# Two output gates of a hybrid block computed as seven half-size products each

## The chip, the cores and the metric

The kernel runs on one core of one Trainium2 chip. The metric is the time of the whole kernel on the device, in microseconds (us), as the median of the runs made. Its engines are named as in the profile: PE is TensorE's matmul, PEld TensorE's weight load, DVE is VectorE, ACT is ScalarE, POOL is GpSimd, SP is SyncE, which here only issues transfers. "ACTq" and "SPq" are the instruction queues of ACT and SP where they issue a transfer.

## The reference

Two blocks are computed on 1024 tokens of width 1024; the change lies in the first, in its forgetting attention and in what follows it.

```python
h = _rmsnorm(x, pre_g)
proj = jnp.einsum('bld,de->ble', h, w_in)
z_ssm, xbc, dt_raw, q, k, v, f_raw, z_att, g_ssm, g_att = jnp.split(proj, _offsets(IN_SPLITS), axis=-1)
...
o = _forgetting_attention(heads(q), heads(k), heads(v), log_f)     # 16 heads of 64
y_att = (o.astype(f32) * jax.nn.silu(z_att.astype(f32))).astype(x.dtype)
p_ssm = jnp.einsum('ble,ed->bld', y_ssm, w_branch_ssm)
p_att = jnp.einsum('ble,ed->bld', y_att, w_branch_att)
merged = jax.nn.sigmoid(g_ssm) * p_ssm + jax.nn.sigmoid(g_att) * p_att
out = jnp.einsum('bld,de->ble', merged, w_out)
return x + _rmsnorm(out, post_g)
```

The two output gates of attention are `silu(z_att)` and `sigmoid(g_att)`, each `h` (1024 x 1024) times 1024 columns of `w_in`.

## The kernel before

**Precision.** Every operand is cut into a rounded high part (ACT) and the rest, the low part (DVE). A product is three matmuls: high x high, high x low, low x high.

**Memory.** On-chip memory is one arena of six regions R(0) to R(5), 8192 fp32 a partition each. `BANK` is 512 columns, `KC` is 8 blocks of 128 rows, `CH` is 4. The accumulators `ps` are 8 banks.

**Two forms of a dense product.** `phase_dense` takes jobs of 512 output columns. A job has 8 steps, one for each block of 128 rows; a step is 8 banks times three matmuls, 24 matmuls. For each step ACT rounds the weights (`_w`, 128x512) and `h` (`_t`, 128x1024), and DVE makes both low parts. `phase_units` computes 1024 columns as a unit of kind "full": seven products of half-size matrices (table `FULL`) instead of eight, in 28 steps of 12 matmuls. Sums of quadrants of `h` (`S1` to `S4`) are not made there: they lie in DRAM (`h_ops`), already cut into high and low, and SP streams one 512 KB operand a step into a ring of four buffers (`bs_a`). `load_operand(n)` waits until step n-4 is multiplied. Raw weights come as four quadrants of 1 MB (`B11`, `B21`, `B12`, `B22`); DVE makes their sums in place (`combine`), ACT rounds one quadrant row block a step (`bs_b`), DVE makes its low part, ACT copies three products out (`take`), and DVE adds four (`join`).

**Order of the stages around the change.** `bs` is a chain of units on TensorE (z_ssm, half of g_ssm, q, the branch of the state-space part, k, v), which ends with v. Its raw weights lie in R(0), its operand buffers in R(5). v is written to DRAM in four quarters by ACT's queue (`att_vh`, `att_vl`). Then comes `phase_forget_attention`: 16 heads of 12 score tiles; heads are loaded ahead by SP (`fa_a` and `fa_b` for a head, `fa_v` for two), ACT makes the exponentials and rounds them (`fa_ph`), POOL makes their low parts (`fa_pl`), TensorE multiplies with `fa_v`. While head h runs, TensorE also computes the row maxima of head h+1 and, from its eighth tile on, of head h+2 (`tops`, matmuls of `fa_a` alone), so `fa_a` of head h+2 is first read in head h. SP's queue does for head h, in this order: load a of head h+2, load b of head h+1, `keep_sums(h-1)`, for even h `load_v`, `spread_inverse(h-2)`.

Regions: `fa_v` and `fa_pl` lie in R(5), so their filling waits for the last product of `bs`. `h` had been in R(0) and was written to DRAM as `hT_kept` (4 MB) in the first stage; at h = 2 SP's queue loads it back into R(0). The stage `za` after attention is one `phase_dense` of six jobs: two for `silu`, two for `sigmoid`, two for the product with `w_branch_att`. All engines run their own instruction lists, written out by this code; nothing reorders them.

The lines that the steps of the prediction touch:

```python
            pool.wait_ge(tail.product, tail.products)      # before fa_v is filled
...
                if h == 2:
                    sp.wait_ge(tail.low, tail.steps)
                    sp.dma_start(hT, hT_kept).then_inc(h_back, 16)
```

## Time and profile before

| what | value |
|---|---|
| median of 3 runs (lowest, highest) | 2888.19 us (2883.37, 2891.59) |
| profiled execution: its time, its span | 2894.49 us, 2892.7 us |
| busy share of the span: PE, PEld | 94%, 77% |
| DVE, ACT, POOL | 68%, 51%, 18% |
| chain that ended last: PE, DMA, DVE, POOL | 51%, 13%, 8%, 6% |

TensorE is busy nearly everywhere, so a microsecond in which it idles or computes less is a microsecond of the kernel, as long as the other engines keep up. Times inside the trace count from the start of the span.

### The profile page before, as it was taken

What the parts mean: (1) busy time and instruction counts of PE and PEld (TensorE: products, weight loads), DVE (VectorE), ACT (ScalarE), POOL (GpSimd) and SP (SyncE); (2) the same over time, 40 slices, a digit from 0 to 9 for tenths busy, and PEclk for the clock granted to TensorE, in tenths of its full rate; (3) what the DMA queues carried; (4) which work ended last, traced back from release to release, by engine and by line L of the source; (5) the groups of instructions that cost most, each with busy time, mean ns of one, the idle gap of its engine ahead of it and who ended that gap; (6) DMA issues with size and microseconds to landing.
All of it is one profiled execution on the core that took longest, in us unless ns stands there. A gap on an engine that the chain in (4) does not pass through costs nothing.

```text
span 2892.7 us, 36287 instructions
## 1 busy us (share of the span) xinstructions
PE 2731.9 (94%) x13214; PEld 2237.7 (77%) x13214; DVE 1961.8 (68%) x2336; ACT 1467.5 (51%) x2228; POOL 519.7 (18%) x394
## 2 busy tenths in 40 slices
PE   7999999999988999999989998999999899999996
PEld 6788978788766777888878877778778788888875
DVE  6776756565654653435544987899763799888885
ACT  5544436443335664443333457533422477777774
POOL 0001400000126773001000000000010044334431
PEclk9999999999999999999999999999999899999998
DMA  5712066743786762121211100112232799999995
GB/s 173 261 49 73 1 194 244 279 157 132 278 243 173 155 137 62 51 102 44 96 58 47 51 23 1 37 44 68 78 104 81 270 381 377 375 362 369 362 360 170
DMA packets 189469, 471.85 MB, mean 163 GB/s; under 512 B 74353, under 2 KB 74481, under 8 KB 164496
## 3 DMA queue, kind: packets, MB, share of 16 engines
q1 hardware_dynamic: 166112, 427.86, 43.5%
q10 hardware_dynamic: 14000, 25.30, 2.4%
q0 software_dynamic: 9216, 16.81, 2.3%
q8 instruction: 89, 1.46, 0.2%
q14 instruction: 52, 0.43, 0.0%
HBM read 410.84 MB, written 75.83 MB: 168 GB/s over the span
## 4 chain that ended last, share of the span: by engine, by line
PE 51%; DMA 13%; DVE 8%; POOL 6%; issue 5%; ACT 4%; SPq 0%; POOLq 0%; DVEq 0%; ACTq 0%; PEldq 0%
PE ps L906 7%; PE ps L908 7%; PE ps L907 7%; DMA ex_raw<-in_w_up_e 6%; POOL fa_pl L1938 6%; DMA ex_raw<-in_w_down_e 5%; PE ps L1354 5%; PE ps L1356 5%; PE ps L1357 5%; PE ps L3515 3%; DVE ex_w L3665 3%; ACT ex_w L3600 2%; PE ps L3243 1%; PE ps L2618 1%; PE ps L2276 1%
## 5 line engine op out<-in xcount | busy, mean ns | idle before, releaser
L3665 DVE TENSOR_TENSOR ex_w<-ex_raw,ex_w 128x2048 fp32r<-128x2048 f32 x190 | 430.6, 2289 | 64.6 <-ACT ex_w L3600 62.3
L3600 ACT ACTIVATE ex_w<-ex_raw 128x2048 fp32r<-128x2048 f32 x190 | 361.9, 1916 | 112.9 <-DMA ex_raw<-in_w_up_e 63.0
L3515 PE MATMUL ps<-ex_w,ex_xT 128*128 128x512 f32 x1536 | 368.0, 396 | 12.6 <-DVE ex_xT L3680 12.3
L3515 PEld LDWEIGHTS ps<-ex_w,ex_xT 128*128 128x128 f32 x1536 | 286.8, 189 | 79.2 <-issue 14.0
L798 DVE SCALAR_TENSOR_TENSOR arena<-arena,small 128x1023 f32<-128x1023 f32 (+9 forms) x168 | 213.4, 1270 | 3.7
L1938 POOL TENSOR_TENSOR fa_pl<-fa_p,fa_ph 128x512 fp32r<-128x512 f32 x192 | 196.3, 1040 | 84.6 <-ACT fa_ph L2040 82.8
L1480 DVE TENSOR_TENSOR bs_b<-arena,bs_b 128x512 fp32r<-128x512 f32 x160 | 110.3, 690 | 139.5 <-ACT bs_b L1378 139.2
L1378 ACT ACTIVATE bs_b<-arena 128x512 fp32r<-128x512 f32 x160 | 100.1, 629 | 201.6 <-PE ps L1357 180.0
L3515 PE MATMUL ps<-ex_w,ex_hT 128*128 128x512 f32 x768 | 184.2, 396 | 1.3 <-issue 1.0
L3515 PEld LDWEIGHTS ps<-ex_w,ex_hT 128*128 128x128 f32 x768 | 142.8, 189 | 31.6 <-issue 2.6
L1755 DVE TENSOR_REDUCE small<-ps 128x1 f32<-128x512 f32 (+1 forms) x192 | 101.1, 553 | 84.6 <-PE ps L1734 56.4
L906 PE MATMUL ps<-gb_t,gb_w 128*128 128x512 f32 x368 | 146.3, 398 | 11.5 <-DVE gb_w L1005 3.7
L1014 DVE TENSOR_TENSOR za_t<-arena,za_t 128x1024 fp32r<-128x1024 f32 x48 | 60.1, 1252 | 142.4 <-ACT za_t L967 142.3
L906 PE MATMUL ps<-za_t,za_w 128*128 128x512 f32 x368 | 145.0, 394 | 5.7 <-DVE za_t L1014 3.3
L2030 ACT ACTIVATE fa_p<-ps 128x512 f32<-128x512 f32 x192 | 94.1, 491 | 101.6 <-PE ps L1972 48.8
L908 PE MATMUL ps<-gb_t,gb_w 128*128 128x512 f32 x368 | 144.6, 393 | 0.0
L907 PE MATMUL ps<-gb_t,gb_w 128*128 128x512 f32 x368 | 144.5, 393 | 0.0
L907 PE MATMUL ps<-za_t,za_w 128*128 128x512 f32 x368 | 144.1, 392 | 0.0
L908 PE MATMUL ps<-za_t,za_w 128*128 128x512 f32 x368 | 143.9, 391 | 0.0
L1354 PE MATMUL ps<-bs_a,bs_b 128*128 128x512 f32 x352 | 138.1, 392 | 4.7 <-DMA bs_a<-h_ops 3.5
L1356 PE MATMUL ps<-bs_a,bs_b 128*128 128x512 f32 x352 | 137.5, 391 | 0.0
L1357 PE MATMUL ps<-bs_a,bs_b 128*128 128x512 f32 x352 | 137.4, 390 | 0.0
(466 smaller groups left out, 6688.8 us busy)
## 6 DMA issues: line engine op xcount, KB each, us to landing
ex_raw<-in_w_gate_e SPq DMA_DIRECT2D x64, 1024.0 KB, 13.8
ex_raw<-in_w_up_e SPq DMA_DIRECT2D x64, 1024.0 KB, 13.6
ex_raw<-in_w_down_e SPq DMA_DIRECT2D x64, 1024.0 KB, 14.1
bs_a<-h_ops SPq DMA_DIRECT2D x100, 512.0 KB, 4.2
arena<-in_w_in SPq DMA_DIRECT2D x72, 512.0 KB, 3.7
arena<-in_w_in SPq DMA_DIRECT2D x18, 1024.0 KB, 6.8
h_ops<-ko_s SPq DMA_DIRECT2D x16, 512.0 KB, 6.1
h_ops<-xbc_t SPq DMA_DIRECT2D x16, 512.0 KB, 4.0
```

What stands on the lines that cost most here:

```text
L798: ins = dve.scalar_tensor_tensor(out=acc[:, b, back:], in0=src[:, b, 0:SEQ - back], scalar=w, in1=acc[:, b, back:], op0=ALU.mult, op1=ALU.add)
L906: nc.tensor.matmul(c.ps[:, t, :], a[0], b[0], start=(k == 0), stop=False)
L907: nc.tensor.matmul(c.ps[:, t, :], a[0], b[1], start=False, stop=False)
L908: mm = nc.tensor.matmul(c.ps[:, t, :], a[1], b[0], start=False, stop=(n == last[j]))
L1354: nc.tensor.matmul(to, w[0], moving[0], start=(k == 0 and fresh), stop=False, skip_group_check=True)
L1356: nc.tensor.matmul(to, w[0], moving[1], start=False, stop=False, skip_group_check=True)
L1357: mm = nc.tensor.matmul(to, w[1], moving[0], start=False, stop=closes, skip_group_check=True)
L1480: tt(b_slot[n % NB][:, 1, :], place_of[rows[u][x][1]][:, k, :], b_slot[n % NB][:, 0, :].bitcast(F32), ALU.subtract).then_inc(low, 1)
L1938: nc.gpsimd.tensor_tensor(low[x % 4][:, 0:w], prob[x % 3][:, 0:w], f32(high[x % 4][:, 0:w]), ALU.subtract).then_inc(lowered, 1)
L3515: mm = nc.tensor.matmul(out, l, r, start=(k == 0 and n == 0), stop=(k == kc - 1 and n == 2))
L3600: nc.scalar.activation(half_of(part[m][0], h), raw[m][:, h * W // 2: (h + 1) * W // 2], ACT.Identity).then_inc(high[m], 1)
L3665: V.tensor_tensor(half_of(part[m][1], h), raw[m][:, h * W // 2: (h + 1) * W // 2], half_of(as_f32(part[m][0]), h), ALU.subtract)\
```

## The change

The four gate jobs of `za` become a new `phase_units` call named `zu` with two full units. Around it:

- `zu` streams its operands from `h_ops`, so `hT_kept` and both its transfers go. Its operand and weight buffers lie in R(0), alternating (`slots`), its raw weights in R(5).
- `fa_v` and `fa_pl` move from R(5) to R(0), the region of the raw weights of `bs`. Filling of `fa_v` now waits for the low parts of the weights of all but the last four steps, and the first `fa_pl` for all of them.
- The four raw quadrants of the first gate are loaded during attention, one at the end of SP's list for h = 4, 6, 8 and 10 (`fetch_za`).
- Steps 0 and 1 of `zu` wait for parts of attention (`slot`, `weights_slot`). The last joins of `zu` are made inside the following `phase_dense` (`open_end`, `UnitsEnd`), which keeps two jobs.
- `y_att` is multiplied by DVE in steps 36 to 43, and `w_out` is loaded in steps 46 to 53 of `zu`, one 512 KB block a step.

```diff
@@ KeptOperands.sync
-        if u == KC + 1:
-            sp.dma_start(self.hT_kept, self.hT).then_inc(self.saved, 16)
@@ phase_units
+    a_at, b_at = slots or (range(NA), range(NA, NA + NB))
+    a_slot = [c.tile(f"{name}_a{s}", region, at_ * 2 * BANK, BANK, F32R, 2) for s, at_ in enumerate(a_at)]
+    b_slot = [c.tile(f"{name}_b{s}", region, at_ * 2 * BANK, BANK, F32R, 2) for s, at_ in enumerate(b_at)]
...
+                if after is not None:
+                    after.slot(sp, n)
                 load_operand(n)
...
+            if after is not None:
+                after.weights_slot(act, n)
...
+        for n in range(NS if open_end else NS + LAG + 2):
@@ phase_forget_attention
-    vh, vl = ([c.named(f"fa_v{n}{s}", 5, (2 * s + n) * TT * VW, TT * VW, F32R)
+    vh, vl = ([c.named(f"fa_v{n}{s}", 0, (2 * s + n) * TT * VW, TT * VW, F32R)
...
-    low = [c.named(f"fa_pl{s}", 5, 4 * TT * VW + s * BANK, BANK, F32R) for s in range(4)]
+    low = [c.named(f"fa_pl{s}", 0, 4 * TT * VW + s * BANK, BANK, F32R) for s in range(4)]
...
                 elif p == 0:
+                    sp.wait_ge(filled, 2)
+                    tail.stored(sp, 2 * tail.splits - 1)
+                else:
                     sp.wait_ge(filled, 4)
-                    tail.stored(sp, 2 * tail.splits - 1)
...
-                if h == 2:
-                    sp.wait_ge(tail.low, tail.steps)
-                    sp.dma_start(hT, hT_kept).then_inc(h_back, 16)
+                fetch(sp, h, tail)
...
-            pool.wait_ge(tail.product, tail.products)
+            pool.wait_ge(tail.low, tail.steps - 4)
...
+                    elif x == 0:
+                        pool.wait_ge(tail.low, tail.steps)
@@ ForgetTail
+    def slot(self, eng, n):
+
+        if n == 0:
+            eng.wait_ge(self.valued, self.tiles * (HEADS - 2) // HEADS)
+        elif n == 2:
+            eng.wait_ge(self.valued, self.tiles)
+
+    def weights_slot(self, eng, n):
+        if n == 0:
+            eng.wait_ge(self.valued, self.tiles * (HEADS - 2) // HEADS)
+        elif n == 1:
+            eng.wait_ge(self.valued, self.tiles)
...
+    def on_sync(self, sp, n):
+        if n == 3:
+            self.keep_sums(sp, HEADS - 1)
+        elif n == 5:
+            self.spread_inverse(sp, HEADS - 2)
+        elif n == 7:
+            self.spread_inverse(sp, HEADS - 1)
@@ _build
+            def fetch_za(sp, h, tail):
+                x = h // 2 - 2
+                if h % 2 == 0 and 0 <= x < 4:
+                    if x == 0:
+                        sp.wait_ge(tail.product, tail.products)
+                    q = ("B11", "B21", "B12", "B22")[x]
+                    sp.dma_start(raw_quad(R(5), q), quad_of(wide_of(w_in, C_ZA), q)).then_inc(za_in, 16)
...
+            GATE, FETCH, FROM = 36, 46, 1
...
+            gates = phase_units(c, "zu", [
+                unit("full", h_ops, wide_of(w_in, C_ZA), True, by_columns(R(1)), ACT.Silu),
+                unit("full", h_ops, wide_of(w_in, C_GA), True, by_columns(R(3)), ACT.Sigmoid)],
+                R(5), 0, within, first=0, at=on_gate_queue, aside=gate_rows, ahead=forgotten.on_scalar,
+                between=lambda pe, n, t, tail: forgotten.on_tensor(pe, n, t), early=za_in,
+                slots=((0, 2, 4, 6), (1, 3, 5, 7)), after=forgotten, open_end=True)
...
-            dense1 = phase_dense(c, "za", [(T(R(0)), wcol(w_in, C_ZA, n), "act_T", wide(1, n), ACT.Silu)
-                                  for n in range(2)]
-                        + [(T(R(0)), wcol(w_in, C_GA, n), "act_T", wide(3, n), ACT.Sigmoid)
-                           for n in range(2)]
-                        + [(T(R(4)), wcol(a["w_branch_att"][0], 0, n), "muladd_T", wide(2, n),
-                            wide(3, n)) for n in range(2)], 5, aside=gate_heads, gated_by=(4, 5),
-                        fetch={1: forgotten.sums, 2: forgotten.inverse, 2 * KC - 1: fetch_out},
-                        beside=split_out, within=within, after=forgotten,
+            dense1 = phase_dense(c, "za", [(T(R(4)), wcol(a["w_branch_att"][0], 0, n), "muladd_T", wide(2, n),
+                            wide(3, n)) for n in range(2)], 5, aside=low_out, ready={0: gated, 1: gated},
+                        beside=split_out, within=within, after=gates_end,
                         halfway=lambda: parts1.low(0))
```

The list of SP inside attention, before, at the end of its part for h = 2 (`hT_kept` is the 4 MB copy of `h`, `fa_a` the rows of a later head):

```order
L1864 DMA att_inverse<-small 128x8
L1869 DMA fa_rinv_8076<-att_inverse 64x1024
L1922 DMA arena<-hT_kept 128x8192
L1679 DMA fa_a_3360<-att_qk 64x2x512
L1681 DMA fa_a_3360<-att_f 2x512
L1682 DMA fa_a_3360<-att_qk 48x2x512
```

The same list after the change, at the end of its part for h = 4:

```order
L1878 DMA att_inverse<-small 128x8
L1883 DMA fa_rinv_8075<-att_inverse 64x1024
L4011 DMA arena<-in_w_in 128x4x512
L1693 DMA fa_a_3357<-att_qk 64x2x512
L1695 DMA fa_a_3357<-att_f 2x512
L1696 DMA fa_a_3357<-att_qk 48x2x512
```

The 4 MB transfer ahead of a head's rows is gone, and a 1 MB quadrant of raw weights stands ahead of the rows of heads 7, 9, 11 and 13.

The list of DVE where attention ends, before (the two copies take the last head out of `ps`):

```order
L2072 COPY arena<-ps 64x512
L2076 COPY small<-ps 1x512
L1005 TENSOR_TENSOR za_w_13112<-arena,za_w_13112 128x512
L1014 TENSOR_TENSOR za_t_13114<-arena,za_t_13114 128x1024
L1879 TENSOR_TENSOR arena<-arena,fa_rinv_8076 128x1024
L1014 TENSOR_TENSOR za_t_13115<-arena,za_t_13115 128x1024
L1005 TENSOR_TENSOR za_w_13113<-arena,za_w_13113 128x512
```

And after:

```order
L2088 COPY arena<-ps 64x512
L2092 COPY small<-ps 1x512
L1490 TENSOR_TENSOR zu_b_13121<-arena,zu_b_13121 128x512
L1893 TENSOR_TENSOR arena<-arena,fa_rinv_8074 128x1024
L1490 TENSOR_TENSOR zu_b_13122<-arena,zu_b_13122 128x512
L1888 RECIPROCAL small<-small 128x8
```

The low part of `h` (`za_t`) no longer stands between the copies and the first matmul; one low part of weights does.

The list of SP in steps 44 to 48 of `zu` after the change, where a block of `w_out` follows each operand from step 46 on:

```order
L1278 DMA zu_a_13117<-h_ops 128x1024
L1278 DMA zu_a_13118<-h_ops 128x1024
L1278 DMA zu_a_13119<-h_ops 128x1024
L4028 DMA arena<-in_w_out 128x1024
L1278 DMA zu_a_13120<-h_ops 128x1024
L4028 DMA arena<-in_w_out 128x1024
L1278 DMA zu_a_13117<-h_ops 128x1024
L4028 DMA arena<-in_w_out 128x1024
```

Before, the eight blocks stood together, between transfers of raw weights for the dense jobs.

## Rows read from the trace of the kernel before

**Rows 1.** Windows: the four gate jobs.

```profile
core 0: us, PE busy (x) PEld busy (x) DVE busy (x) ACT busy (x) POOL busy (x), PEclk, DMA share, GB/s
1120.50:1299.10 178.60, 177.33 (x768) 145.47 (x769) 69.87 (x76) 67.35 (x96) 0.00 (x0) 0.99 0.23 74
```

**Rows 2.** Window of seven products of streamed operands (28 steps), PE alone.

```profile
385.44:461.60 76.16, 76.16 (x338) 1.00 0.74 252
```

**Rows 3.** Timeline where attention ends and the gate jobs begin and end.

```profile
1120.54 0.76 PE L906 MATMUL ps<-za_t,za_w 128*128 128x512 f32 x1 [3.28 <-DVE za_t L1014]
...
1118.64 0.67 DVE L1005 TENSOR_TENSOR za_w<-arena,za_w 128x512 fp32r<-128x512 f32 x1
1119.24 1.21 DVE L1014 TENSOR_TENSOR za_t<-arena,za_t 128x1024 fp32r<-128x1024 f32 x1
...
1299.12 0.47 PE L906 MATMUL ps<-za_t,za_w 128*128 128x512 f32 x1 [0.30 <-PE ps L908]
```

**Rows 4.** PE's waits for POOL in attention: total, times, longest.

```profile
PE ps L1997 <- POOL fa_pl L1938: 8.7, 22, 0.9
```

**Rows 5.** Timeline where `bs` ends and attention begins, five engines.

```profile
848.05 0.80 PE L1992 MATMUL ps<-fa_ph,fa_v 128*128 128x512 f32 x1 [6.94 <-DMA fa_v<-att_vl]
...
834.10 0.54 POOL L1929 MEMSET fa_v<- 128x512 f32 x1 [51.68 <-PE ps L1357]
841.08 1.26 POOL L1938 TENSOR_TENSOR fa_pl<-fa_p,fa_ph 128x512 fp32r<-128x512 f32 x1 [5.05 <-ACT fa_ph L2040]
...
836.05 1.00 SPq L1905 DMA_DIRECT2D fa_v<-att_vh  x2
798.37 22.01 SPq L1278 DMA_DIRECT2D bs_a<-h_ops  x9
...
813.39 0.53 ACTq L1431 DMA_DIRECT2D att_vl<-bs_low  x1
842.99 0.52 ACT L2040 ACTIVATE fa_ph<-fa_p 128x384 fp32r<-128x384 f32 x1 [1.72 <-DMA att_vh<-bs_high]
```

**Rows 6.** Transfers: KB each, median us from issue to landing; below, `fa_b`.

```profile
bs_a<-h_ops SPq DMA_DIRECT2D x100, 512.0 KB, 4.2
arena<-in_w_in SPq DMA_DIRECT2D x18, 1024.0 KB, 6.8
att_vl<-bs_low ACTq DMA_DIRECT2D x4, 1024.0 KB, 7.8
arena<-hT_kept SPq DMA_DIRECT2D x1, 4096.0 KB, 15.4
small<-att_sums SPq DMA_DIRECT2D x16, 4.0 KB, 1.6
...
DMA to landing us min/median/max: 5.1/6.4/16.2
```

**Rows 7.** Timeline of the reload of `h` and of TensorE behind it.

```profile
895.10 1.22 SPq L1922 DMA_DIRECT2D arena<-hT_kept  x1
...
912.43 0.48 PE L1726 MATMUL ps<-fa_a 128*128 128x128 f32 x1 [9.55 <-DMA fa_a<-att_qk]
```

**Rows 8.** Timeline, PE: first score of heads 3, 4 and 15.

```profile
894.17 0.39 PE L1962 MATMUL ps<-fa_a 128*128 128x512 f32 x1
...
921.08 0.39 PE L1962 MATMUL ps<-fa_a 128*128 128x512 f32 x1
...
1101.10 0.39 PE L1962 MATMUL ps<-fa_a 128*128 128x512 f32 x1
```

**Rows 9.** Timeline: the rows of head 7, issued and first read.

```profile
938.33 0.60 SPq L1679 DMA_DIRECT2D fa_a<-att_qk  x1
...
945.76 0.22 PE L1726 MATMUL ps<-fa_a 128*128 128x128 f32 x1
```

**Rows 10.** PE's waits in the whole stage `bs`; DVE joins one product.

```profile
PE ps L1354 <- DMA bs_a<-h_ops: 4.7, 3, 2.1
...
831.97 2.73 DVE L1500 TENSOR_TENSOR arena<-arena,ps 128x512 f32<-128x512 f32 x4 [1.84 <-PE ps L1357]
```

More of the change, by code:

```diff
@@ L1182, in phase_units @@
 def phase_units(c, name, units, weights_at, region, within, first=0, begin=None, aside=None, beside=None,
-                middle=None, at=None, fill=None, needs=None, early=None, between=None, ahead=None):
+                middle=None, at=None, fill=None, needs=None, early=None, between=None, ahead=None, slots=None, after=None,
+                open_end=False):
     nc = c.nc
@@ L1287, in load_later @@
                         load_weights(u, q)
-        load_operand(0)
-        load_operand(1)
+        for n in range(2):
+            if after is not None:
+                after.slot(sp, n)
+            load_operand(n)
         for n in range(NS + 8):
             if 2 <= n < NS:
+                if after is not None:
+                    after.slot(sp, n)
                 load_operand(n)
@@ L1375, in round_weights @@
             weights_landed(act, u, q)
+            if after is not None:
+                after.weights_slot(act, n)
             if makes(n):
@@ L1431, in store, with follow @@
                         act.dma_start(to_low, units[u].other[1](r, s).bitcast(F32)).then_inc(low_kept[i % 2], 16)
-        for n in range(NS + LAG + 2):
-            if n < NS:
-                round_weights(n)
-            store(n)
-            if ahead is not None:
-                ahead(n)
+        def follow(n):
             m = n - LAG
@@ L1444, in _ @@
                 finish(m)
+        tail.rest_scalar = lambda i: follow(NS + i)
+        for n in range(NS if open_end else NS + LAG + 2):
+            if n < NS:
+                round_weights(n)
+            store(n)
+            if ahead is not None:
+                ahead(n)
+            follow(n)
             if beside is not None:
@@ L1514, in finish, with follow @@
                                        op1=ALU.subtract).then_inc(split_low, 1)
-        for n in range(NS + LAG + 2):
-            if n + 1 < NS:
-                combine(n + 1)
-            if n < NS:
-                low_weights(n)
+        def follow(n):
             m = n - LAG
@@ L1526, in _ @@
                 finish(m)
+        tail.rest_vector = lambda i: follow(NS + i)
+        for n in range(NS if open_end else NS + LAG + 2):
+            if n + 1 < NS:
+                combine(n + 1)
+            if n < NS:
+                low_weights(n)
+            follow(n)
             if aside is not None:
@@ L2141, in on_vector, with __init__, sync, weights @@
             self.invert(HEADS - 2)
-        elif n == 2:
+        elif n == 5:
             self.invert(HEADS - 1)
-        elif n == 5:
+        elif n == 9:
             self.norm(HEADS // 2 - 1)
     def on_scalar(self, n):
-        if n == 2 * KC:
+        if n == 14:
             self.nc.scalar.wait_ge(self.normed, HEADS // 2)
+class UnitsEnd:
+    def __init__(self, tail, retired):
+        self.tail, self.retired = tail, retired
+    def sync(self, sp):
+        sp.wait_ge(self.retired, 1)
+        sp.wait_ge(self.tail.low, self.tail.steps - 4)
+    def weights(self, act):
+        act.wait_ge(self.retired, 1)
+        act.wait_ge(self.tail.low, self.tail.steps - 4)
+    def scalar(self, act):
+        pass
+    def tensor(self, pe, t):
+        if t == 0:
+            pe.wait_ge(self.retired, 1)
+            pe.wait_ge(self.tail.joined, self.tail.early_joins)
+        elif t >= 4:
+            pe.wait_ge(self.tail.joined, self.tail.joins - 7 + t)
+    def on_vector(self, n):
+        if n == 1:
+            self.tail.rest_vector(2)
+    def on_scalar(self, act, n):
+        if n == 0:
+            act.wait_ge(self.tail.low, self.tail.steps)
+        elif n == 1:
+            self.tail.rest_scalar(3)
 class MergedParts:
@@ L3853, in _build @@
         with c.stage() as (alive, block):
-            first, second = (alive.enter_context(Scope(nc)) for _ in range(2))
+            first, second, units = (alive.enter_context(Scope(nc)) for _ in range(3))
             retired = [c.sem(alive, f"retired{n}") for n in range(2)]
-            ctx, within = first, (first, block)
+            units_retired = c.sem(alive, "units_retired")
+            ctx, within = units, (units, block)
             forget = ForgetSums(c, ctx, decays, R(1))
@@ L3970, in gate_heads, with low_out @@
+            c.retire(block, units, [(forgotten.valued, forgotten.tiles), (forgotten.taken, 2 * HEADS),
+                                    (gates.low, 1)], units_retired)
+            gates_end = UnitsEnd(gates, units_retired)
+            def low_out(n, tapped, by_act, by_vec, moved):
+                gates_end.on_vector(n)
+                if n == 2:
+                    nc.vector.wait_ge(gates.opened, 32)
                 k, odd = divmod(n - FROM, 2)
@@ L3973, in gate_heads @@
                     nc.vector.tensor_tensor(out_low[k], out_raw[k], out_high[k].bitcast(F32), ALU.subtract)
-            def fetch_out(sp):
-                sp.wait_ge(gated, 1)
-                for k in range(KC):
-                    sp.dma_start(out_raw[k], a["w_out"][0][k * P:(k + 1) * P, :])\
-                        .then_inc(wo_in[k], 16)
             def split_out(n, tapped, by_act):
-                forgotten.on_scalar(n)
+                gates_end.on_scalar(nc.scalar, n)
                 k, odd = divmod(n - FROM, 2)
                 if not odd and 0 <= k < KC:
+                    if k == 0:
+                        nc.scalar.wait_ge(gates.product, gates.products)
                     nc.scalar.wait_ge(wo_in[k], 16)
```

89 lines of the change are left out of this document (39 added, 50 removed).

## The prediction, made before the changed kernel ran

> **What bounds the kernel now.** I read the page first: TensorE is busy 94% of the span and no other engine above 68%, so the end is set by what TensorE computes and by the few places where it stands still. Then I read the windows of the stages that the change touches, then TensorE's waits in them, then the timeline at each large wait.
>
> The four gate jobs take 178.6 us for 768 matmuls, and TensorE is busy in 177.3 of them [rows 1]. DVE works 70 us there and ACT 67: the stage is bound by the number of matmuls. A stretch of streamed seven-product work in `bs` shows what the new form costs: 28 steps of 12 matmuls, 336, in 76.16 us without a gap at full clock (the row counts two more at its edges), so 0.2267 us a matmul and 2.72 us a step [rows 2]. In it operands arrive from DRAM at 252 GB/s and TensorE does not wait.
>
> Attention has two large waits besides many small ones for POOL, 8.7 us in 22 [rows 4]. The first is at its start: `bs` ends at 833.8, POOL fills the constant parts of `fa_v` only then, at 834.10, SP issues the loads of v at 836.05, and the first product with v begins at 848.05, after 6.94 us of idling [rows 5]. The second is in head 3: the reload of `h`, 4 MB, is issued at 895.10, just ahead of the rows of head 5, and TensorE waits 9.55 us for these, until 912.43 [rows 7]. Both are transfers that come late, and both lie where the change moves something.
>
> **The gates as units.** Removed: 768 matmuls. Added: 14 products of 48, 672. At 0.2267 us these are 174.1 and 152.3 us. The jobs took 178.6 us from the first matmul at 1120.54 to that of the job behind them at 1299.12 [rows 3]; 4.5 of it is a slow start at the low clock and the changes of job. I keep half, 2.3, for the new stage, since it also starts after a short idle time: 154.6, a gain of 24.0.
>
> The start comes earlier too. The last head's copies end at 1118.6; DVE then makes a low part of weights (0.67 us) and one of `h` (1.21), and the first matmul follows at 1120.54 [rows 3]. The second of the two goes, since streamed operands arrive already cut; ACT's rounding of the first weights waits for 14 of 16 heads only. I take 1.1 us of gain, the time between the starts of that low part and the matmul less what a semaphore takes. Together 25.1.
>
> What must stay hidden: one operand a step. It is issued when step n-4 is done, so it has three steps, 8.2 us, and 512 KB land in 4.2 in the median [rows 6]. At the change from the first gate to the second four quadrants of 1 MB are mixed in, and in steps 46 to 53 eight blocks of `w_out`. In all of `bs`, with most of its 18 quadrants and 100 streamed operands [rows 6], operands cost TensorE 4.7 us in three waits [rows 10]. DVE's worst place is steps 36 to 39: four low parts and eight sums at 0.67, a join of 2.73, four of the multiplications by the gate at 1.21, in sum 15.6 us against 10.9 of TensorE. The eight steps 36 to 43 make 23.1 against 21.8. With four weight buffers DVE may be up to three steps ahead, 8.2 us, which covers an excess of 4.7. Without that cover it would be 4.7 us of stall. The last joins stand behind the first two steps' operands of the dense stage, and its first four banks (2.7 us of work) are free by then, so the seam costs nothing; the changes of bank of a job, before, cost more. Bounds for the stage: a gain of 27.4 (nothing of the 4.5 stays) down to 15.7 (both stalls, 9.4, come in full). I take 25.1, because the rows of the same code run at 2.72 without a gap.
>
> **The start of attention.** POOL's filling now waits for the low parts of the weights before the last product, which DVE makes before TensorE multiplies them. The loads of v also wait for two quarters of v in DRAM: the second is issued at 813.39 and lands 7.8 later, 821.2, while SP is free after its last operand at 820.4 [rows 5, 6]. So v is requested near 821 instead of 836 and is there before 834. What is late next? The first product with v wants POOL's first low part, 841.08 plus 1.26; the second wants ACT's second rounding block, which today ends a wait for a store of v at 842.99, and then a POOL low part near 844.9. Today that second product ends its wait behind the first, near 851.2 (848.05 plus six matmuls and a score). I take the difference, 6.3. Bounds: 4, if ACT's and POOL's chain for the first head is later than I place it, and 8, if the store lands earlier because v is no longer loaded beside it.
>
> **The reload of `h`.** It goes. Its write in the first stage goes too; I cost that at nothing, since no engine reads what it writes until attention and the dense jobs beside it are bound by matmuls. From the start of head 3 to that of head 4 are 26.91 us; the 11 heads behind take 180.02, 16.37 each [rows 8]. The difference, 10.5, is the wait and the half clock after it. Bounds 9.5 (the wait alone) and 11.0 (if the heads that I compare with hold half a microsecond each of waits for POOL [rows 4] which head 3 had not).
>
> **The quadrants in attention.** Four transfers of 1 MB now stand ahead of the rows of heads 7, 9, 11 and 13. The 4 MB took 15.4 us and a 4 KB transfer takes 1.6, so 1 MB occupies the engines for (15.4 - 1.6) / 4 = 3.45 us [rows 6]. The rows of head 7 are issued at 938.33 and first read at 945.76, 7.43 us later, without a wait [rows 9]; a comparable load, `fa_b`, lands in 5.1 at best [rows 6]. That leaves 2.3 us of slack, so each costs 1.1 us, four cost 4.4. The even heads' rows have more room, since SP waits for the scores of an earlier head there and not for its own list. Bounds: nothing, if the transfers overlap, and 12, if each costs what a lone 1 MB transfer shows over a small one, 6.8 - 1.6 - 2.3 = 2.9.
>
> The Trainium skill, page "DMA: Bandwidth & Descriptors", section "Anatomy of one DMA — SWDGE (gpsimd) path", puts a transfer at some 2.0 us plus its bytes over 436 GB/s; by that 1 MB would occupy 2.4 us and all four quadrants would fit the slack within 0.1 each, which makes the whole 4 us faster than my sum. This case's 4 MB row, at 304 GB/s without its fixed part, does not agree, and the page's fit is for another queue than SP's; the row decides.
>
> **Sum.** -25.1 - 6.3 - 10.5 + 4.4 = -37.5 us. The sum is made against the profiled execution, span 2892.7, time 2894.49; the median of the runs is 6.3 lower. I take the same difference from the median: 2888.2 - 37.5 = 2850.7, about 1.3%. A measurement here tells 0.3%, 8.7 us, from no change.
>
> **Rivals.**
> 1. *The quadrants cost in full.* Each stall of 2.9 us comes, and the clock falls behind some: 12 to 16 us instead of 4.4. For it: the odd heads' rows have 2.3 us of slack and nothing else in SP's list to fill it. Against: nothing else is under way then. With 14 us in place of 4.4 that is 2860.
> 2. *The units stall.* Operands and DVE in steps 20 to 53 cost the 9.4 us named above on top of the sum. For it: four quadrants and the full operand stream together, where `bs` had held operands. Against: rows 2. 2860.
> 3. *The stall at the start moves.* ACT's wait for the last store of v, and POOL behind it, keep the first head late, and only about 1 of the 6.3 us is won. For it: the store is issued after `bs` ends in both kernels. Against: its wait ends at 842.99, 5 us before v does. 2856.
> 4. *The quadrants are hidden.* The first rows of the head behind land in the slack; 2846.
> 5. *Slower than before.* The ring of four operands falls behind in every step. The three other gains are 12.4 us net, so the gates would have to lose what they gain and that: a step of 2.72 + 37.5/56 = 3.39 us. That needs a landing of about 10 us on average, three steps, for 512 KB, against a median of 4.2. The point from which it decides is a landing of 8.2; beyond it each microsecond costs a third of one a step, 19 us in all. 2895 or more.
> 6. *It does not do what it says.* Fewer products, but TensorE idles for DVE or DRAM by as much: within 8.7 us of before. For it only that DVE's work per matmul grows.
>
> **Chances.** The forecast as summed, with its own range of 2844 to 2856: 0.53. Rival 1: 0.14. Rival 2: 0.11. Rival 3: 0.08. Rival 4: 0.06. Rival 5: 0.03. Rival 6: 0.05. The range reaches over rivals 1 to 4 and, on the low side, to the sum of the good bounds (27.4 + 8 + 11.0 = 46.4, 2842) with little to spare; the high end, 2866, takes in rivals 1 and 2 at once less a part. Faster 0.92, same 0.05, slower 0.03.
>
> **What would show each step.** The new profile should have 672 matmuls of `zu` in about 155 us, with a step of 2.72 in the middle of both gates; a wait of TensorE on `zu_a` or on DVE's `zu_b` that sums to more than 2 us speaks for rival 2. At the start of attention the wait for `fa_v` should be gone and the first product with v follow the end of `bs` by about 8 us instead of 14.2. Head 3 should take 16 to 17 us. TensorE's waits for `fa_a` should be four, of about 1 us, in heads 5, 7, 9 and 11; none is rival 4, and 3 us each is rival 1. I am wrong above all if the operand ring starves, which would stand in TensorE's waits on `zu_a` in every product, or if the start of attention, where five engines hand over at once, has a chain that I did not see.

## The result and the profile after

The changed kernel takes 2864.01 us in the median of 4 runs (2859.96 to 2864.7); the kernel before 2888.12 (4 runs, 2883.37 to 2891.59). The ratio is 0.9915, with a 95% interval from 0.9898 to 0.9932: 24 us faster, of 37.5 forecast. The profiled execution has a span of 2862.8 us.

I read the new trace at the same marks as the old one: the end of `bs`, the first score of heads 3, 4 and 15, the first matmul of the gates and that of the job behind them. First the timeline of TensorE at these marks. A row gives the start and the length of an instruction in us; in brackets, at its end, stand the idle time before it and what ended that:

```profile
890.68 0.39 PE L1978 MATMUL ps<-fa_a 128*128 128x512 f32 x1
...
907.65 0.39 PE L1978 MATMUL ps<-fa_a 128*128 128x512 f32 x1
...
1098.46 0.39 PE L1978 MATMUL ps<-fa_a 128*128 128x512 f32 x1
...
1116.74 0.77 PE L1358 MATMUL ps<-zu_a,zu_b 128*128 128x512 f32 x1 [2.14 <-DVE zu_b L1490]
```

Against [rows 8]: head 3 takes 16.97 us instead of 26.91. Head 4 to head 15 take 190.81 instead of 180.02.

The windows of the changed kernel, from the end of `bs` (830.93) to head 3, from head 4 to the last product with v (1114.28), and the two gates:

```profile
core 0: us, PE busy (x) PEld busy (x) DVE busy (x) ACT busy (x) POOL busy (x), PEclk, DMA share, GB/s
830.93:890.68 59.75, 51.33 (x260) 38.69 (x259) 30.47 (x56) 35.26 (x78) 34.48 (x34) 0.86 0.69 156
907.65:1114.28 206.63, 191.06 (x1046) 143.71 (x1044) 109.57 (x204) 130.57 (x302) 149.91 (x147) 0.98 0.64 148
...
1116.74:1271.92 155.18, 155.18 (x672) 128.30 (x673) 88.78 (x132) 66.77 (x110) 0.00 (x0) 0.98 0.70 245
```

The same two stretches of attention before:

```profile
833.59:894.17 60.58, 49.45 (x260) 37.38 (x259) 30.49 (x56) 35.07 (x78) 36.27 (x38) 0.89 0.74 166
921.08:1116.94 195.86, 188.00 (x1046) 140.71 (x1044) 109.46 (x204) 130.39 (x301) 149.76 (x147) 1.00 0.61 135
```

So the trace answers in these terms. The start of attention gains 0.8 us; head 3 gains 9.9; heads 4 to 15 lose 10.8; the gates start 2.47 us after the last product with v instead of 3.60 and then take 155.18 us, in which the window shows no idle time, against 178.58 [rows 1], together 24.5. The sum, 0.8 + 9.9 - 10.8 + 24.5 = 24.4 us, is close to the difference of the medians, 24.1. The span of this one execution is 29.9 shorter. Of the other 5 us half lie before the end of `bs`, which is 2.7 us earlier, and half behind the gates (from 1271.92 to the end 1590.9 us, before 1593.6). I don't count either as an effect: the end of `bs` lies between 829.0 and 836.0 in the kernels below, whose `bs` is the same, and at 834.2 in the one that still writes `hT_kept`.

Two terms are off, both in attention. TensorE's and ACT's waits from 834 to 1112 us in the changed kernel (total, times, longest):

```profile
ACT fa_p L2046 <- DMA att_shifts<-fa_shift: 13.2, 4, 3.7
PE ps L2008 <- ACT fa_ph L2056: 10.9, 5, 5.3
PE ps L2013 <- POOL fa_pl L1954: 8.9, 20, 0.9
ACT fa_ph L2056 <- DMA att_vh<-bs_high: 7.7, 1, 7.7
PE ps L1740 <- DMA fa_a<-att_qk: 2.1, 3, 0.9
```

TensorE's 6.94 us for `fa_v` [rows 5] and 9.55 for `fa_a` [rows 7] are gone. In their place stands ACT, which waits for two DMAs of its own, and TensorE behind it; the rows of keys and queries that I had watched, `fa_a`, cost 2.1 us in all.

**The first of the two waits**, at the start of attention; the timeline of SP, ACT, POOL and TensorE:

```profile
822.61 5.49 SPq L1921 DMA_DIRECT2D fa_v<-att_vl  x2
828.15 2.51 SPq L1693 DMA_DIRECT2D fa_a<-att_qk  x1
...
834.30 1.05 SPq L1921 DMA_DIRECT2D fa_v<-att_vh  x2
835.39 10.52 SPq L1921 DMA_DIRECT2D fa_v<-att_vl  x2
...
834.49 0.37 ACTq L1436 DMA_DIRECT2D att_vh<-bs_high  x1
846.27 0.52 ACT L2056 ACTIVATE fa_ph<-fa_p 128x384 fp32r<-128x384 f32 x1 [7.67 <-DMA att_vh<-bs_high]
...
838.40 1.27 POOL L1954 TENSOR_TENSOR fa_pl<-fa_p,fa_ph 128x512 fp32r<-128x512 f32 x1 [28.51 <-ACT fa_ph L2056]
...
838.47 0.77 PE L2008 MATMUL ps<-fa_ph,fa_v 128*128 128x512 f32 x1
846.85 0.69 PE L2008 MATMUL ps<-fa_ph,fa_v 128*128 128x384 f32 x1 [5.26 <-ACT fa_ph L2056]
```

The first product with v follows the end of `bs` by 7.5 us instead of 14.5, as forecast. But the last store of v, issued at 834.49, lands 11.8 us later. Before, ACT's wait for it ended at 842.99 [rows 5], 5.8 us after its issue:

```profile
837.15 0.41 ACTq L1430 DMA_DIRECT2D att_vh<-bs_high  x1
```

SP, now early, has issued keys and queries of heads 1 and 2 ahead of the store (from 828.15 on; before the change they came at 840.01, behind it), and the values of heads 2 and 3 at the same moment as the store and right behind it. The packets by queue (q1 is SP's, q10 ACT's; packets, MB, share of 16 engines), from 834.9 to 838:

```profile
q1 hardware_dynamic: 294, 0.69, 106.3%
```

And from 842 to 846.2:

```profile
DMA packets 1433, 1.63 MB, mean 388 GB/s; under 512 B 732, under 2 KB 732, under 8 KB 1432
...
q10 hardware_dynamic: 716, 1.43, 88.2%
q1 hardware_dynamic: 716, 0.18, 19.1%
```

In the first of the two stretches the only queue that moved a packet is SP's; the store moves in the second.

**The second**, in head 5, behind the first quadrant; SP, ACT and TensorE:

```profile
924.29 0.59 SPq L4011 DMA_DIRECT2D arena<-in_w_in  x1
924.92 0.58 SPq L1693 DMA_DIRECT2D fa_a<-att_qk  x1
...
937.53 0.34 SPq L1873 DMA_DIRECT2D small<-att_sums  x1
...
932.16 0.27 ACTq L1785 DMA_DIRECT2D att_shifts<-fa_shift  x1
937.89 0.24 ACTq L1790 DMA_DIRECT2D fa_b<-att_shifts  x1
938.22 0.60 ACT L2046 ACTIVATE fa_p<-ps 128x512 f32<-128x512 f32 x1 [3.58 <-DMA att_shifts<-fa_shift]
...
932.85 0.33 PE L1740 MATMUL ps<-fa_a 128*128 128x128 f32 x1 [0.41 <-DMA fa_a<-att_qk]
939.39 0.50 PE L2008 MATMUL ps<-fa_ph,fa_v 128*128 128x512 f32 x1 [1.83 <-ACT fa_ph L2056]
940.74 0.50 PE L2013 MATMUL ps<-fa_pl,fa_v 128*128 128x512 f32 x1 [0.62 <-POOL fa_pl L1954]
...
942.30 0.63 PE L2010 MATMUL ps<-fa_ph,fa_v 128*128 128x512 f32 x1
```

The rows of head 7 are only 0.41 us late. What is late is a store of 4 KB, the shift of the next head (made of the row maxima of its scores): ACT writes it at 932.16 and reads it back with a second DMA, and waits between the two with all its exponents behind it. Then TensorE idles 1.83 and 0.62 us, and its next products with v take 0.63 us and not 0.40: the clock has fallen to half. From 932.3 to 935.9 the packets are all SP's, with the engines full:

```profile
DMA packets 292, 0.81 MB, mean 225 GB/s; under 512 B 40, under 2 KB 40, under 8 KB 292
q1 hardware_dynamic: 292, 0.81, 107.8%
```

The 225 GB/s here are not the rate of the quadrant, which is issued at 924.29 and has landed 6.4 us later; they are the rate of the rows of keys and queries behind it. The kernel before shows much the same (220 GB/s) with no quadrant there, in head 5 from 939 to 947.4. While the quadrant's own packets pass, from 927 to 930 in the changed kernel, the rate is 379 GB/s. First before, then after:

```profile
DMA packets 794, 1.85 MB, mean 220 GB/s; under 512 B 113, under 2 KB 118, under 8 KB 793
...
DMA packets 568, 1.14 MB, mean 379 GB/s; under 512 B 16, under 2 KB 16, under 8 KB 567
```

ACT waited for this store before the change too, in the same head. There it had no slack to give, and the quadrant came on top:

```profile
945.63 0.27 ACTq L1771 DMA_DIRECT2D att_shifts<-fa_shift  x1
...
949.50 0.60 ACT L2030 ACTIVATE fa_p<-ps 128x512 f32<-128x512 f32 x1 [1.37 <-DMA att_shifts<-fa_shift]
```

### The profile page after: what moved, and what is told of

Same layout as the page of the kernel before. It is cut to its first block, busy times and chain, and to the rows that moved or that the text cites. A ratio compares the mean times of both kernels' runs of the same rounds, so it can differ in the third digit from the quotient of the medians.

```text
span 2862.8 us, 36318 instructions
## 1 busy us (share of the span) xinstructions
PE 2703.6 (94%) x13108; PEld 2216.0 (77%) x13118; DVE 1980.0 (69%) x2392; ACT 1465.8 (51%) x2244; POOL 521.2 (18%) x394
## 4 chain that ended last, share of the span: by engine, by line
PE 51%; DMA 14%; DVE 8%; POOL 5%; issue 5%; ACT 4%; POOLq 0%; SPq 0%; DVEq 0%; ACTq 0%; PEldq 0%
DMA ex_raw<-in_w_up_e 8%; PE ps L1358 7%; PE ps L1361 6%; PE ps L1360 6%; PE ps L906 5%; PE ps L908 5%; PE ps L907 5%; POOL fa_pl L1954 5%; DMA ex_raw<-in_w_down_e 3%; PE ps L3569 3%; DVE ex_w L3719 3%; ACT ex_w L3654 2%; PE ps L3297 1%; PE ps L2330 1%; PE ps L3299 1%
## 5 line engine op out<-in xcount | busy, mean ns | idle before, releaser
L906 PE MATMUL ps<-xbc_t,xbc_w 128*128 128x512 f32 x320 | 126.7, 396 | 7.5 <-DVE xbc_t L1014 4.2
L967 ACT ACTIVATE gb_t<-arena 128x1024 fp32r<-128x1024 f32 x48 | 50.9, 1061 | 158.0 <-PE ps L908 144.6
L2919 POOL TENSOR_TENSOR arena<-arena 128x1024 f32<-128x1024 f32 x3 | 8.6, 2878 | 657.8 <-DVE arena L2874 537.0
L907 PE MATMUL ps<-xbc_t,xbc_w 128*128 128x512 f32 x320 | 125.6, 393 | 0.0
```

What stands on the lines that cost most here:

```text
L906: nc.tensor.matmul(c.ps[:, t, :], a[0], b[0], start=(k == 0), stop=False)
L907: nc.tensor.matmul(c.ps[:, t, :], a[0], b[1], start=False, stop=False)
```

## The experiments

Twelve kernels beside the two; each was timed in four to six runs, beside runs of the kernel before, and one run of each was profiled. I read them by the same stretches. "Start" is from the end of `bs` to head 3, "head 3" to head 4, "heads 4 to 15" to the last product with v, all in us from each trace; R is the ratio to before with its interval, "time" the median.

| kernel | start | head 3 | heads 4 to 15 | time | R |
|---|---|---|---|---|---|
| before | 60.6 | 26.9 | 195.9 | | 1 |
| changed | 59.8 | 17.0 | 206.6 | 2864.0 | 0.9915 (0.9898, 0.9932) |
| v1_later | 56.7 | 17.1 | 210.0 | 2864.7 | 0.9906 (0.9892, 0.9921) |
| quads_odd | 57.7 | 15.8 | 205.9 | 2859.2 | 0.9889 (0.9872, 0.9905) |
| fill_late | 59.9 | 16.1 | 209.3 | 2866.5 | 0.9911 (0.9896, 0.9926) |
| no_reload | 60.4 | 16.7 | 197.1 | 2879.4 | 0.9958 (0.9945, 0.9972) |
| quads_last | 59.7 | 16.6 | 196.7 | 2851.8 | 0.9879 (0.9861, 0.9898) |
| halves | 57.0 | 16.8 | 204.5 | 2857.7 | 0.9911 (0.9894, 0.9927) |
| fetch_later | 59.2 | 15.9 | 205.2 | 2854.0 | 0.9893 (0.9876, 0.9909) |
| held_loads | 53.8 | 15.8 | 208.3 | 2856.4 | 0.9901 (0.9883, 0.9918) |
| held_last | 54.0 | 15.9 | 195.9 | 2846.4 | 0.9847 (0.9828, 0.9867) |
| held_last_fetch | 53.9 | 15.8 | 197.1 | 2844.5 | 0.9827 (0.9805, 0.9849) |
| held_fill_late | 58.9 | 16.8 | 210.6 | 2861.9 | 0.9900 (0.9882, 0.9918) |
| quads_behind | 57.7 | 15.8 | 208.5 | 2858.6 | 0.9902 (0.9880, 0.9924) |

The medians come from five sets of runs, in which before took 2883.4 to 2890.3, so kernels are compared by R. Its intervals reach some 5 us to either side. The same edit shows how far a stretch of one profile can be trusted: with the quadrants at the end of the even heads, heads 4 to 15 take 206.6 to 210.6 us in five kernels; the start with SP's loads in the order of the change takes 57.0 to 59.8 in six (the changed kernel's 59.8 is the longest of them).

**The reload alone.** The kernel before with a reload of 16 columns of `h` in place of all of it (its gates then compute with the rest of the region as it stands):

```diff
-                    sp.dma_start(hT, hT_kept).then_inc(h_back, 16)
+                    sp.dma_start(hT[:, 0:16], hT_kept[:, 0:16]).then_inc(h_back, 16)
```

> The kernel before with one edit: the reload of h brings 16 of 8192 columns, 8 KB instead of 4 MB. It leaves out most of that copy, so the gates are computed from whatever lies in the region. Theory (the reload stood ahead of the rows of head 5): TensorE's wait of 9.5 us for fa_a goes, head 3 takes 16 to 17 us instead of 26.9, the whole 10 to 11 us faster than before, 2877 to 2878. Rival (part of the 10.5 us comes back later, since POOL and the other loads fall behind anyway): 5 us or less, 2883.

Head 3 falls to 16.7 us, and the median lies 10.9 us under that of before (2890.3), where the ratio's interval reaches from 8 to 16. That term is right.

**The start: what is ahead of the store.** First only the values of heads 2 and 3, from head 0 to head 1:

```diff
-                if h % 2 == 0 and h + 2 < HEADS:
+                if h == 1:
+                    load_v(1)
+                elif h and h % 2 == 0 and h + 2 < HEADS:
                     load_v(h // 2 + 1)
```

> The changed kernel with one edit: the values of heads 2 and 3 are loaded at h = 1 of SP's list instead of h = 0. Theory (transfers that SP has issued ahead hold up the last store of v on ACT's queue, and ACT's rounding waits for it): the store, which took 11.8 us from 834.49, no longer has 1 MB of 256-byte pieces beside it; ACT's wait of 7.7 us shrinks to 3 or less, TensorE's wait of 5.3 us for fa_ph goes or shrinks below 1.5, head 1 starts 25 us or less after head 0 instead of 27.9; the whole 3 to 5 us faster than the changed kernel, about 2860. Rival (the store is slow by itself, DRAM writes late in the stage): it still lands 11 to 12 us after its issue and nothing moves, 2864.

ACT's wait fell from 7.7 to 5.0 us and TensorE's longest to 2.6. But that wait is 5.5 us in `halves`, with the loads in the order of the change, the stretch, 56.7, is hardly outside the spread of the others, and the time did not move. Nothing is settled by this run. So the next one takes away all that stands ahead, and adds to the edit above:

```diff
             load_v(0)
+            tail.all_stored(sp)
             for h in range(HEADS):
```

> The changed kernel where SP, once the values of heads 0 and 1 are issued, waits for the last store of v before it issues keys and queries of heads 1 and 2, and loads the values of heads 2 and 3 in head 1. If the store is late because SP's loads are ahead of it on the DMA engines, it lands 5 to 7 us after its issue as before (5.8), not 11.8 (with only the values' loads moved it was 9.0), ACT's wait at the start of attention falls from 7.7 to under 2 us, and the stretch from the last product to head 3, 59.8 us in the changed kernel, to 54 to 56, if the loads then are not late themselves: time 2859 to 2861. If the store is slow for another reason (its own 256-byte pieces, the loads of the values of heads 0 and 1 at 821 to 828), it lands at 10 us or more again, everything behind it is late too, and the time is 2864 to 2868.

The timeline of ACT and TensorE there:

```profile
834.34 0.37 ACTq L1436 DMA_DIRECT2D att_vh<-bs_high  x1
...
838.67 0.53 ACT L2059 ACTIVATE fa_ph<-fa_p 128x384 fp32r<-128x384 f32 x1 [0.25 <-DMA att_vh<-bs_high]
...
846.05 0.33 PE L1740 MATMUL ps<-fa_a 128*128 128x128 f32 x1 [1.47 <-DMA fa_a<-att_qk]
```

The store is in DRAM within 4.3 us (its packets are of 2 KB, 1.43 MB in 716 above, and not of 256 bytes as I wrote), ACT's wait is 0.25, and the start takes 53.8 us: 6.8 less than before, where my sum had 6.3. It is 54.0 and 53.9 in the two other kernels with this edit. The price of it, keys of head 2 that are 1.47 us late, is in that number. The time alone would not show the gain: R is 0.9901 against 0.9915, and the intervals overlap. Is the move of the values to the other region needed for this? POOL made to wait for the whole product again:

```diff
-            pool.wait_ge(tail.low, tail.steps - 4)
+            pool.wait_ge(tail.product, tail.products)
```

> The changed kernel with the filling of fa_v put back behind the last product of the chain before attention, as it was before the change; regions stay as changed. Theory (the early loads of v moved the stall and did not remove it): head 1 starts as late after head 0 as before, 28.7 us against 27.9 now, the whole 0 to 1 us slower, 2864 to 2866. Rival (the early filling is worth most of the 6.3 us that were forecast, and the profile of the changed kernel caught a bad case): 5 to 6 us slower, 2870.

> The changed kernel with SP held for the last store and the values of heads 2 and 3 in head 1, but POOL again waits for the whole product before it sets ones and zeros, so that the values of heads 0 and 1 are loaded as late as before the change. If the move of the values' place is worth 6 us once the store is no longer in the way, the stretch from the last product to head 3 is 59 to 61 us instead of 53.8, and the time 5 to 7 us over that of the held kernel with the early fill (2860 to 2866 here). If the order of the loads alone did it and the move nothing, it is 54 to 55.

With the loads in the order of the change the early fill is worth nothing that can be told (59.9 against 57.0 to 59.8, the same ratio). With SP held the traces put it at 5.1 us (58.9 against 53.8), and TensorE waits 5.3 us for `fa_v` again. The times do not bear this out: R is 0.9900 with the late fill and 0.9901 with the early one, where 5.1 us would be 0.0018. So the wait that returns is shown, and what it costs the whole kernel is not. Two waits end near each other there, and each hides what the cure of the other is worth.

**The quadrants: are they the loss?** All four in head 14, where SP's list is short:

```diff
-                x = h // 2 - 2
-                if h % 2 == 0 and 0 <= x < 4:
-                    if x == 0:
-                        sp.wait_ge(tail.product, tail.products)
-                    q = ("B11", "B21", "B12", "B22")[x]
+                if h == 14:
+                    sp.wait_ge(tail.product, tail.products)
+                for q in ("B11", "B21", "B12", "B22") if h == 14 else ():
```

> The changed kernel with all four quadrants of the attention gate's weights fetched in head 14, where the trace of the changed kernel shows SP's queue empty from 1092 to 1102 us. From head 4 to the last value matmul before took 195.9 us, the changed kernel 206.6 (10.8 more). If that excess is the price of the quadrants beside the heads' own transfers, that stretch goes back to 195.5 to 198 us, and the time falls by 8 to 11 us, to 2853 to 2856 (ratio to before 0.987 to 0.9885). If it comes from something else that the change did in these heads (the order on SP, the place of the values), the stretch stays at 206 and the time at 2864. If 4 MB in one piece hold up the small transfers of head 14 and 15 or the gates' first operands, these heads or the first gate matmul come 3 to 8 us later, and the time is 2857 to 2861.

Its window from head 4 to the last product with v:

```profile
910.85:1107.59 196.74, 188.14 (x1046) 140.84 (x1044) 109.50 (x204) 130.68 (x302) 150.24 (x147) 1.00 0.66 155
```

The loss is gone: 196.7 us as before the change, at the full clock. Against 206.63 us of the changed kernel, 2.9 us of the difference are TensorE's busy time, for as many matmuls (188.14 against 191.06), which is the fallen clock, and 7.0 are idle. The gates start 2.47 us after the last product as they did. The quadrants in these heads are the whole of this loss. R falls from 0.9915 to 0.9879, with intervals that just touch.

**Which property of them?** Three kernels: in the odd heads; there too, but behind the rows of keys and queries; and in eight halves of 512 KB. The edits are in `fetch_za`. The first is that of `quads_odd` and `quads_behind`; `quads_behind` also moves the call, from the end of the loop's body to the line behind `load_b(h + 1)`. Of the second, of `halves`, the heart is shown (the gate also waits for eight transfers in place of four):

```diff
-                x = h // 2 - 2
-                if h % 2 == 0 and 0 <= x < 4:
+                x = (h - 1) // 2 - 2
+                if h % 2 and 0 <= x < 4:
```

```diff
...
+                x, r = h // 2 - 2, h % 2
...
+                    rows = slice(CH // 2 * r, CH // 2 * (r + 1))
+                    sp.dma_start(raw_quad(R(5), q)[:, rows], quad_of(wide_of(w_in, C_ZA), q)[:, rows])\
+                        .then_inc(za_in, 16)
```

> The changed kernel with the four 1 MB quadrants at h = 5, 7, 9, 11 instead of 4, 6, 8, 10, so ahead of the rows of even heads, which had 4.6 us of slack against 2.2, and not behind a load of v. Theory (a quadrant costs because it stands in one line with the head's rows and with the small transfers of the shift behind it): the waits on fa_a go, and the waits on fa_ph that follow the late shift go or halve; heads 4 to 12 together take 5 to 9 us less, 2857. Rival (the cost is the bytes themselves, wherever they stand, since attention's transfers fill the engines to two thirds): heads 4 to 12 take as long as in the changed kernel within 2 us, 2864.

> The changed kernel with the four quadrants in heads 5, 7, 9 and 11, issued right behind the rows of keys and queries of that head instead of at the end of the head before, ahead of them. Same bytes, same number of heads; what changes is what stands behind the quadrant: the sums and the 4 KB store of the shift, no rows. Theory of the slack (the loss is that the rows behind a quadrant are late): the stretch from head 4 to the end of attention falls to 198 to 201 us. Theory of the bytes (the engines have no room in these heads, whatever the order; eight halves gave 204.5, the end of the odd heads 205.9, the end of the even ones 206.6 to 210): 204 to 208, with ACT's longest wait for the shift's store at 4 us or more, and the time within 3 us of 2860.

> The changed kernel with the quadrants in eight halves of 512 KB, one in each of heads 4 to 11, instead of four of 1 MB in the even ones. Theory of the slack (a piece costs what it is longer than the slack of the loads behind it, 2.1 to 2.9 us in odd heads, 4.6 in even ones, at 2.4 us a MB): a half takes 1.2 us and fits everywhere, the stretch from head 4 to the end of attention falls from 206.6 to 196 to 199 us, the time to 2854 to 2858. Rival, a price by the byte (the engines are full in these heads, and what is added to them comes back in full, 2.7 us a MB): the stretch stays at 205 to 209 and the time within 3 us of 2864.

None of them comes near 196. Halves that should have fitted every slack still cost 8.6 us (their ratio, 0.9911, is that of the changed kernel), and with nothing but small transfers behind the quadrant until the next head's rows `quads_behind` loses 12.6. Its waits from head 4 on, where TensorE waits for `fa_a` nowhere, and its window:

```profile
ACT fa_p L2046 <- DMA att_shifts<-fa_shift: 13.9, 6, 3.6
PE ps L2013 <- POOL fa_pl L1954: 7.7, 19, 0.9
PE ps L2008 <- ACT fa_ph L2056: 5.2, 4, 1.8
...
906.74:1115.24 208.50, 195.11 (x1046) 145.04 (x1044) 109.56 (x204) 130.42 (x302) 149.78 (x147) 0.97 0.63 147
```

So it is not the slack of the rows. What has grown is ACT's wait for the shift, 13.9 us against 7.9 before the change. `quads_odd` has a better ratio than the changed kernel (0.9889 against 0.9915), but the intervals overlap, and its heads 4 to 15 are within 1 us of the changed kernel's; I don't rank the places inside the heads.

**ACT's wait.** The second DMA of the shift two steps later in ACT's order:

```diff
-                    elif i == TT - EARLY + 4 and h + 1 < HEADS:
+                    elif i == TT - EARLY + 6 and h + 1 < HEADS:
```

> The changed kernel with ACT's fetch of the next head's shift two steps later in its order (9 instead of 7), so that its wait for the 4 KB store comes some 2.7 us later. If ACT's waits for that store (13.2 us in 4, up to 3.7) are what passes the quadrants' delay on to the matmuls, these waits fall below 5 us in all, and the stretch from head 4 to the end of attention shortens by 4 to 7 us (to 200 to 203), time 2857 to 2860. If the loads of keys and queries themselves are late (PE's waits for them), or PE would have stood anyway, it stays within 2 us of 206.6 to 210, and the time within 2 us of 2864. If the row of shifts now lands too late for the first score of the next head, the heads become longer, and the time is 2868 or more.

ACT's waits for the shift fell from 13.2 to 1.5 us and TensorE's for ACT went away, but its waits for `fa_a` rose from 2.1 to 9.7 us:

```profile
PE ps L1740 <- DMA fa_a<-att_qk: 9.7, 4, 5.4
ACT fa_p L2046 <- DMA att_shifts<-fa_shift: 1.5, 2, 0.9
```

The stretch of this trace is 205.2: where ACT no longer stood still for the shift, the rows were late instead. So ACT's wait is one way for the loss to reach TensorE, and not the only one. How much the later fetch won stays open. The profiled run was the slowest of its four (2865.7 us, the others 2852.9 to 2854.6), and the ratio, 0.9893, lies between those of the changed kernel and of `quads_last`, with an interval that overlaps both.

**Both cures, and ACT's fetch.** `held_loads` and `quads_last` together, and these with the later fetch:

> The two cures together: SP waits for the last store of v before it issues keys and queries of heads 1 and 2, and all four quadrants are fetched in head 14. If the two costs are separate, as the stretches say (start 59.8 to 53.8 us, heads 4 to 15 206.6 to 196.7), the stretches are 53.8 and 196 to 197.5 here too, the ratio to before is 0.9875 less 5.5 to 6.5 us, 0.985 to 0.9865. If they share something (what the start gains is lost in the first heads, as its loads are later), the start or head 1 to 4 is 3 us or more longer and the ratio 0.987 or more.

> The same with the fetch of the shift two steps later in ACT's order. Without quadrants in the heads ACT still waits for its 4 KB store (7.9 us in 5 with the quadrants last), up to 2.2. If these waits cost the matmuls something, the stretch from head 4 to the end of attention goes from 196.7 to 193 to 195, the ratio 0.0005 to 0.001 lower than that of its neighbour. If they lie beside the matmuls, no change (within 1 us). If the later fetch makes the next head's first score late, 198 or more.

The stretches add as they should, 54.0 and 195.9. `held_last` is at 0.9847: 1.5% under before, and its interval lies below those of the changed kernel and of `held_loads`, so the move of the quadrants shows in the time too. Against `quads_last` the intervals overlap by a hair, so what SP's hold wins is clear in the traces and only likely in the time. The later fetch changes no stretch by more than 1.3 us; the intervals of the two overlap, and I count them the same.

## Why the prediction was right, and where it was not

**Right in mechanism and size.** The gates: 154.6 us forecast, 155.18 measured, no wait on `zu_a`, and 2.1 us for DVE before the first matmul; start and stage gave 24.5 of 25.1. The ring never starved, though DMA ran at 245 GB/s through the stage, so rivals 2 and 5 are out; and what follows the gates got no longer, as the seam at no cost had it. The reload: 9.9 in the changed kernel, 10.2 when taken away alone, of 10.5.

**The range held in part by luck.** 2864.0 lies outside 2844 to 2856, which I gave 0.53, and 2 us inside the high end of the whole range. That end was meant for rivals 1 and 2 together; what came is nearer to rivals 1 and 3 together (2850.7 + 9.6 + 5.3 = 2865.6), a pair to which I gave no chance.

**Wrong: "the first product with v ... Today that second product ends its wait behind the first ... I take the difference, 6.3."** The term was 0.8 in the changed kernel, and 0.8 to 3.6 in the six kernels with this order of loads. The step that failed is the one before it: I left the store's landing at its old time, 842.99, and even let it land earlier "because v is no longer loaded beside it". The early fill freed SP's whole list, not only the load I looked at. Two heads' keys and queries went ahead of the store and two more heads' values beside it, and it landed at 846.27. Rival 3 named this wait; what it lacked was what makes it longer. The 6.3 is real in the traces, as `held_loads` shows with 6.8, but only in another order.

**Mis-sized: the quadrants, 4.4 forecast, 10.8 measured** (8.6 to 14.7 in the nine kernels that fetch them in heads 4 to 11, against 195.9). My end of "12, if each costs what a lone 1 MB transfer shows" was nearer. The price of a megabyte was about right: by the windows the 16 engines are busy for 0.61 of 195.86 us before and for 0.64 of 206.63 after, 12.8 us more, so 3.2 us for each quadrant (an estimate from these shares, good to half a microsecond), where I had 3.45. What failed is the slack that I took from it. I charged the quadrants to the rows of keys and queries alone, with 2.3 us of slack, and these rows indeed cost little (0.41 us in head 5, 2.1 us in three waits in all). But a 4 KB store on another queue, with the whole of ACT behind it, stood behind the same bytes, and it had no slack: ACT waited 1.37 us for it in that head before the change and 3.58 after. The clock then added 2.9 us, which I had only in rival 1. So rival 3 came in the changed kernel and most of rival 1 with it. They are what makes the forecast 13 us too good: 6.3 - 0.8 and 10.8 - 4.4 are 11.9, and 1.2 more are in gates and reload.

The rule of the Trainium skill that I weighed (page "DMA: Bandwidth & Descriptors", section "Anatomy of one DMA — SWDGE (gpsimd) path") puts a megabyte at an estimated 2.4 us. The trace's 3.2 us is nearer to the row's 3.45 than to that, so the row decided rightly. Neither price would have shown the loss, as the error lay in the slack.

## What to carry to other kernels

When a wait on the queue that issues the loads is moved forward, everything behind it in that queue moves forward too; list it, and ask which store or small round trip on another queue now stands behind these bytes. Before you take slack off the price of an added transfer, list every wait behind its bytes, on the other queues too, and look first for the shortest round trip that an in-order engine waits for. If that engine already waits before the change, there is no slack, and the transfer costs about its full price. Where two waits end close together, curing one shows nothing; try both before calling either worthless.

## What the runs showed of the hardware

A 4 KB store on ACT's queue, alone on it, was issued at 932.16 and had moved no packet by 935.9, while the 16 engines worked off 292 packets of SP's queue; its 16 packets came in the 1.6 us after that (the queues from 935.9 to 937.5), among the last of SP's. In the kernel before the same store, issued at 945.63, moved none by 946.9, while 78 packets of SP's passed. In both the separate queue was no way past the bytes already handed to the engines; what differs is how many these were. First the changed kernel, then the one before from 945.6 to 946.9:

```profile
q1 hardware_dynamic: 39, 0.07, 24.0%
...
q10 hardware_dynamic: 16, 0.00, 2.7%
...
q1 hardware_dynamic: 78, 0.27, 101.1%
```

The Trainium skill says (page "DMA: Bandwidth & Descriptors", section "Queues, rings and completion order") that each engine turns from one queue's ring to the next after a packet of some 9 to 17 descriptors, at most 64. The trace does not contradict it: some 18 of its packets an engine (292 / 16) passed before the other queue had a turn, and before the change some 5 (78 / 16). That these packets are the page's descriptors is not shown here.

Full engines moved 225 GB/s (before the change 220) when rows of keys and queries were the work, 379 GB/s with the quadrant, and 388 GB/s when the store of v was most of it (842 to 846.2 us). Why the rows are slower is not shown.

TensorE's granted clock fell from the 2.4 GHz level to the 1.2 GHz one in head 5, between 941 and 942 us, right behind the idle times of 1.83 and 0.62 us. The mean of the granted clock (the third number from the end) is 0.50 from 942 to 943, the lower of the two levels:

```profile
942.00:943.00 1.00, 1.00 (x3) 0.81 (x3) 0.62 (x2) 0.58 (x2) 1.00 (x2) 0.50 0.00 0
```
